# Moving the tiles of a four-block float32 kernel to 1,024-byte starts in SBUF

## What is computed

```
first_block: h = rms_norm(x); x = x + hybrid_mixer(h)   # state-space mixer and attention, w_in 1024 x 7440
             h = rms_norm(x); x = x + hier_moe(h)       # 4 groups of 8 experts, 1024 -> 256 -> 1024
             x = x + sigmoid(rms_norm(x) @ w_ple_gate) * (p @ w_ple)
then:  layer 0  short convolution mixer, FFN            # FFN: silu(h @ w1) * (h @ w3) @ w2, 1024 -> 2816 -> 1024
       layer 1  neighbourhood attention, FFN
       layer 2  long (Hyena) convolution mixer, FFN
       layer 3  short convolution mixer, FFN, last norm
```

## Time and profile before

| What | Value |
|---|---|
| Median of three timed runs | 1972.4 us |
| Profiled execution, its own time | 1969.42 us |
| Profiled execution, span | 1967.6 us |
| TensorE busy | 1894.0 us, 13,360 matmuls |
| VectorE busy | 1375.0 us |
| ScalarE busy | 921.0 us |
| GpSimd busy | 46.4 us |
| Moved by DMA | 365.97 MB, 186 GB/s over the span |
| Granted TensorE clock, mean | 0.991 of full speed |

### The profile page before, as it was taken

The page is one execution under the profiler, slowest core; times in us unless marked ns, Lnnn a source line. Parts: engine busy times, 40 slices in busy tenths (PEclk is TensorE's granted clock), DMA queues, the critical chain, the costliest instruction groups (busy, mean ns, idle before and its releaser), DMA issues.

```text
span 1967.6 us, 32453 instructions
## 1 busy us (share of the span) xinstructions
PE 1894.0 (96%) x13360; PEld 1729.2 (88%) x13360; DVE 1375.0 (70%) x1577; ACT 921.0 (47%) x991; POOL 46.4 (2%) x65
## 2 busy tenths in 40 slices
PE   6999998899999979999999999999989999999999
PEld 6998888788888769999989899987879999999998
DVE  4777977766777666666667666678997666676665
ACT  4544745555666553433345453334334333444332
POOL 0000000000000000001101000000000000000000
PEclk8999999999999989999999999999999999999999
DMA  6553343786788747555554385552324555555553
GB/s 216 175 172 101 127 144 150 262 307 265 287 303 306 255 141 195 186 192 192 192 171 130 108 254 193 191 190 88 108 82 154 188 192 193 176 193 172 192 192 107
DMA packets 243771, 365.97 MB, mean 186 GB/s; under 512 B 12550, under 2 KB 217817, under 8 KB 231257
## 3 DMA queue, kind: packets, MB, share of 16 engines
q1 hardware_dynamic: 243673, 364.58, 54.9%
HBM read 363.50 MB, written 1.05 MB: 185 GB/s over the span
## 4 chain that ended last, share of the span: by engine, by line
PE 83%; DVE 10%; ACT 2%; issue 2%; DMA 2%; SPq 1%; POOL 0%; DVEq 0%; ACTq 0%
PE proj L960 40%; PE proj L1522 11%; PE acc L1294 11%; PE proj L979 7%; PE acc L1486 5%; DVE ring_lo L2506 2%; ACT ring_hi L1935 1%; PE acc L1307 1%; DMA raw<-in_w_in_dram 1%; PE proj L1789 1%; PE acc L1004 1%; PE proj L1628 1%; PE misc L1467 0%; PE acc L1586 0%; PE acc L1111 0%
## 5 line engine op out<-in xcount | busy, mean ns | idle before, releaser
L2506 DVE TENSOR_TENSOR ring_lo<-raw,ring_hi 128x2048 fp32r<-128x2048 f32 x242 | 560.0, 2317 | 213.5 <-ACT ring_hi L1935 212.3
L1935 ACT ACTIVATE ring_hi<-raw 128x2048 fp32r<-128x2048 f32 x242 | 462.3, 1914 | 441.6 <-PE proj L960 205.9
L960 PE MATMUL proj<-h_hi,ring_hi 128*128 128x256 f32 x1424 | 407.3, 286 | 10.2 <-DVE ring_lo L2506 10.0
L960 PE MATMUL proj<-h_lo,ring_hi 128*128 128x256 f32 x1424 | 396.0, 278 | 0.0
L960 PE MATMUL proj<-h_hi,ring_lo 128*128 128x256 f32 x1424 | 395.9, 278 | 0.0
L960 PE MATMUL proj<-g_hi,ring_hi 128*128 128x256 f32 x1088 | 303.0, 279 | 1.2 <-DVE g_lo L2550 1.2
L960 PE MATMUL proj<-g_lo,ring_hi 128*128 128x256 f32 x1088 | 301.8, 277 | 0.0
L960 PE MATMUL proj<-g_hi,ring_lo 128*128 128x256 f32 x1088 | 301.8, 277 | 0.0
L960 PEld LDWEIGHTS proj<-h_hi,ring_hi 128*128 128x128 f32 x1424 | 268.3, 188 | 21.9 <-DVE ring_lo L2506 11.2
L960 PEld LDWEIGHTS proj<-h_lo,ring_hi 128*128 128x128 f32 x1424 | 269.3, 189 | 3.8 <-issue 2.9
L960 PEld LDWEIGHTS proj<-h_hi,ring_lo 128*128 128x128 f32 x1424 | 268.4, 189 | 0.0
(11 more groups left out here) (451 smaller groups left out, 3423.7 us busy)
## 6 DMA issues: line engine op xcount, KB each, us to landing
raw<-in_f_w_dram SPq DMA_DIRECT2D x132, 1024.0 KB, 5.0
raw<-in_w_in_dram SPq DMA_DIRECT2D x29, 1024.0 KB, 5.4
raw<-in_w_exp_gate_dram SPq DMA_DIRECT2D x25, 1024.0 KB, 5.0
raw<-in_w_exp_up_dram SPq DMA_DIRECT2D x24, 1024.0 KB, 4.8
raw<-in_a_w_in_dram SPq DMA_DIRECT2D x24, 1024.0 KB, 5.1
raw<-in_w_exp_down_dram SPq DMA_DIRECT2D x23, 1024.0 KB, 5.9
raw<-in_b_w_qkv_dram SPq DMA_DIRECT2D x12, 1024.0 KB, 5.1
raw<-in_c_w_in_dram SPq DMA_DIRECT2D x12, 1024.0 KB, 5.1
```

The costliest lines, as they stand in the source:

```text
L960: last = pe.matmul(bank[:, a, :], w[:, k, a * P:(a + 1) * P], h[:, k, :], start=(k == 0 and w is hi and h is h_h and (a == 0 or not first) ...
L1935: act.activation(w_hi[n.slot][:, :], raw[n.slot][:, :], ACT.Copy).then_inc(hi_ready, 1)
L2506: dve.tensor_tensor(w_lo[n.slot][:, :], raw[n.slot][:, :], w_hi[n.slot][:, :].bitcast(f32), SUB)\
```

## The change

The small tiles (`ssq` to `inv_b`) are asked for first instead of between and behind the large ones. A tile `fill` of 192 bytes, which nothing reads or writes, brings the allocator to byte 20,480. From there on every large tile has a size that is a multiple of 1,024 bytes, so `raw`, `ring_hi`, `ring_lo`, `x_res`, `h_hi`, `h_lo` and the work area's base all begin at a multiple of 1,024. The work area becomes 192 bytes shorter, and the four tiles that reached near its end are put 128 or 64 bytes lower in it.

| Tile | start before | past a multiple of 1,024 | start after | past a multiple of 1,024 |
|---|---|---|---|---|
| raw0 (raw1, raw2 behind it) | 16,512 | 128 | 20,480 | 0 |
| ring_hi | 41,088 | 128 | 45,056 | 0 |
| ring_lo | 65,664 | 128 | 69,632 | 0 |
| x_res | 90,240 | 128 | 94,208 | 0 |
| h_hi, h_lo | 98,624, 106,816 | 320 | 102,400, 110,592 | 0 |
| work0 | 118,592 | 832 | 118,784 | 0 |
| g, hid, own (whole KB in the work area), raw_spare | | 832 | | 0 |
| second_hi, second_lo | | 832 | | 896 |

```
+        ssq, ms, inv, neg_half, eps_col, ident, ones, params, inv_b    # the same sb(...) lines, moved here
+        sb("fill", [P, (20 * 1024 - nc.sbuf_base) // 4])
         raw = [sb(f"raw{i}", [P, CHUNK]) for i in range(RING)]
         ring_hi = sb("ring_hi", [P, RING, CHUNK], f32r)
         ring_lo = sb("ring_lo", [P, RING, CHUNK], f32r)
...
         x = sb("x_res", [P, TT, D])
-        ssq, ms, inv, neg_half, eps_col                                # stood here
         h_hi = sb("h_hi", [P, KT, SEQ], f32r)
         h_lo = sb("h_lo", [P, KT, SEQ], f32r)
-        ident, ones, params, inv_b                                     # stood here
...
-        sets_hi = [ring_hi, at("second_hi", [P, RING, CHUNK], 60 * KB, f32r)]
-        sets_lo = [ring_lo, at("second_lo", [P, RING, CHUNK], 84 * KB, f32r)]
+        sets_hi = [ring_hi, at("second_hi", [P, RING, CHUNK], 60 * KB - 128, f32r)]
+        sets_lo = [ring_lo, at("second_lo", [P, RING, CHUNK], 84 * KB - 128, f32r)]
...
-        ys = at("ys", [P, 2, 2, SEQ], 102 * KB)
-        z_t = at("z_t", [P, 2, SEQ], 106 * KB)
+        ys = at("ys", [P, 2, 2, SEQ], 102 * KB - 64)
+        z_t = at("z_t", [P, 2, SEQ], 106 * KB - 64)
```

More of the change, by code:

```diff
@@ L344, in sem @@
             return ctx.enter_context(nc.semaphore(name))
+        ssq = sb("ssq", [P, TT, 2])
+        ms = sb("ms", [P, TT])
+        inv = sb("inv", [P, TT])
+        neg_half = sb("neg_half", [P, 16])
+        eps_col = sb("eps_col", [P, 1])
+        ident = sb("ident_sb", [P, P])
+        ones = sb("ones", [P, P])
+        params = sb("params", [P, PARAM_TILES * P])
+        inv_b = sb("inv_b", [P, SEQ])
+        sb("fill", [P, (20 * 1024 - nc.sbuf_base) // 4])
         raw = [sb(f"raw{i}", [P, CHUNK]) for i in range(RING)]
@@ L352, in build @@
         x = sb("x_res", [P, TT, D])
[L353 to L357, removed]
         h_hi = sb("h_hi", [P, KT, SEQ], f32r)
         h_lo = sb("h_lo", [P, KT, SEQ], f32r)
[L360 to L363, removed]
         work0 = -(-nc.sbuf_base // 32) * 32
```

## The result

The change made the kernel slower. Four timed runs of the changed kernel have a median of 2010.99 us (2009.19 to 2013.76) against 1973.39 us for the kernel before; the ratio is 1.0185, with a 95% interval of 1.0162 to 1.0207. That is 38 us more, where no change, 1970 us in a range of 1953 to 1985, had been forecast.

A forecast was written before the change was run, and what follows sets the result against it. TensorE was taken to bound the kernel, with 83% of the chain of waits. 1969.4 + 0.5 - 1.0 = 1968.9 us against the profiled execution, stated as 1970 us, no change, in a range of 1953 to 1985.

The forecast's parts named there:

- TensorE, which of the two rates: FFN and projection matmuls: 117.8 or 113.4 ns comes from falling in step after the last stall, not from starts; 0 us.
- The rival of the common start: Weights and tokens starting alike modulo 1,024 make the slower rate the rule in FFN rounds; +21 us, 1993 us; chance 0.10.
- Its +4.0 us for the pieces of 24: In L1294, 36 pieces of 24 matmuls of 512 columns would go from 5.49 to 5.60 us.
- The 1 ns of the expert rows: Expert down product: weights read from the second set cost 1 ns more each than from the ring; taken as +0.5 us.
- its two readings: Second set dearer for sharing its start with `hid` (+2.4 us), or for starting 64, not 128, past 256 (-0.6 us).
- VectorE and ScalarE at 0: Subtractions and other work on these engines keep their durations, 2290 ns a subtraction, wherever operands start; 0 us.
- DMA, -1.0 us in a range of 0 to -2.0: Aligned loads move faster where the chain waits on them, 19.6 us of moving; the middle of both ends was taken.
- the bound of 0.3 us: If each of 290 VectorE subtractions won or lost 10 ns, 2.9 us of its time, 0.3 us would be on the path.

The follow-up runs named there:

- micro3: Matmuls alone, 256 columns, token starts in steps of 4 bytes, other matmuls run between products; at distance 192, 117.8 or 113.3 ns a matmul.
- before_split: Kernel before with one plain float32 matmul of 256 columns (`spread_inv`) made two of 128, addresses unchanged; 1970.03 us, ratio 0.9985.
- rel192: Changed kernel with the five smallest tiles back in front of h, so tokens start 192 bytes past the weights modulo 256; 1971.12 us, ratio 0.9995.
- rel64: Changed kernel with 64 bytes put in front of h, so h and the work area start 64 past a multiple of 1,024; 1998.24 us, ratio 1.0143.
- tok112: Kernel before with weights at a multiple of 256 and h and g 112 bytes behind them modulo 256; 1971.61 us, ratio 0.9991.
- micro1: Matmuls alone, no loads or other engines, 44 pairs of weight and token starts; 113.3 to 120.0 ns for 256 columns.

## Why the prediction was wrong

**The step that failed** is "TensorE, which of the two rates": "Starts need not touch this: I take 0". Starts set the rate. The observation under it was right, that the same addresses show both rates and that it hangs on what ran before; micro3 shows exactly that, and before_split does for the heads of the FFNs. The conclusion was not: a history that picks one of two rates at one distance doesn't mean that all distances have the same two. At distance 0 there is only one, 120.0 ns, and it is worse than both.

**The rival of the common start was the right mechanism, and was priced too low and held too unlikely** (0.10, 1993 us). Its price was taken from the slowest rate that the trace showed, 117.8 ns, as if that were the worst there could be. 36 pieces rose by 0.60 us and not by 0.41, and the pieces that were at 117.8 already, counted as nothing, rose too: the 528 of layer 0 by 1.16 us, each head of 144 by 0.31. Its +4.0 us for the pieces of 24 had the wrong sign: they went from 5.49 to 5.47. The argument against it was also wrong. `h` and `g` lie 192 and 704 bytes behind the ring modulo 1,024, and that both show the same rates was read as two different distances agreeing. Modulo 256 both are 192. They were one point, and that point was the best of the four. The rival's word for the period, 1,024, was the diff's and not the trace's.

**The 1 ns of the expert rows** was read as a hint that a common start is dear. Neither of its two readings held. By the first, a common start is dear, the ring's product should have got slower; it got faster (1176 to 1169 ns for the three kinds). By the second, 64 past a multiple of 256 is dear, the second set's should have got faster; it got slower (1179 to 1184). Measured alone, 512 columns take 226.7 ns at 0 against 229 at 192; and the rival carried the hint to 256 columns. The term was put at +0.5 us. The mean distances between starts in the two traces (L1294 229.3 to 227.9 ns, L1522 229.3 to 230.5, L1486 230.4 to 229.8) make it about -0.5: small, as forecast, with the other sign.

**VectorE and ScalarE at 0** held: 2289 ns. The 290 subtractions of the bound are those into the ring; with the second set's there are 338, and the bound of 0.3 us stays.

**DMA, -1.0 us in a range of 0 to -2.0**, could not be told from nothing in the time: rel192 gives a ratio of 0.9995. Its three loads on the chain take 13.69, 5.96 and 6.87 us against 13.68, 6.09 and 6.80, together 0.05 us less. Hidden, as the prediction said, there is a small gain: the FFN's loads land in 4.8 to 4.9 us in the median in the four kernels whose raw buffers start at a multiple of 256 (after, rel64, rel192, tok112) and in 5.0 to 5.1 in the others. From the split at 256-byte boundaries that the Trainium skill describes (DMA: Bandwidth & Descriptors, How a descriptor splits into AXI transactions) the prediction had the estimate that each load's moving part would get 11% shorter; the runs bear out 2 to 4% of the time to landing, and nothing on the chain.

The cause that is shown is the distance: one line brings the loss into the kernel before, 192 bytes take it out of the changed one, and matmuls alone have the same rates. That the two that meet are the stream of one matmul and the weight load of the next is argued, not shown, from the fact that nothing else ran in micro1. The Trainium skill, SBUF — State Buffer, section Who interferes with whom, calls TensorE's two read ports independent. No run here looks at the ports themselves, but a rate of fp32r matmuls that differs by 6% with nothing but the distance of the two operands does not sit easily with that. Why the rates are 16 cycles apart, why 112 was good with weights at a multiple of 256 and not with weights 80 past one, and what makes a long piece such as the 528 take one rate or the other, stays open.

## What to carry to other kernels

Before tiles are moved in SBUF, write down for each hot matmul how far the start of one operand lies behind that of the other, modulo 256 bytes, and keep it; a layout that is tidier may be the worst one. Where a tuned kernel's rate is at one of several levels, a table of matmuls alone over the distances takes one run of 0.6 ms and tells whether the level can still fall. A piece that got faster can leave the next one in a slower step, so read the chain behind the edit too.

## What the runs showed that was not expected

For fp32r matmuls of 256 columns with the tokens streaming, back to back in the order of `product_f`, the time of one after a pause is 113.3, 117.8, 118.7 or 120.0 ns at distances of 192, 64, 128 and 0 bytes modulo 256, with the weights at a multiple of 256 or 128 past one. For 512 columns it is 226.7 at 0, 229 at 192 and 233 at 64. At distance 192 one plain float32 matmul of 256 columns in front leaves the run at 117.8 ns, and one or two of 128 columns leave it at 113.3; in the kernel, 24 matmuls of 512 columns at 226.7 ns leave it at 117.8 and the same 24 at 229 leave it at 113.3. Steps of 4 bytes change the rate, with single good values at 112 and 192. A start at a multiple of 1,024 gave the loads, the copies and the subtractions nothing that the kernel's time can show.
